# First layer's input projections: queries and keys ahead, then the convolution, then values; heads and latent convolution finished between the blocks

## The reference, cut to what matters

```python
def even_mixer(h_lat, h_ctx, w_in, conv_w, q_g, k_g, rpb, w_out, need_ctx):
    def query_side(p):
        gb, gc, u, q = jnp.split(p, [CONV_CH, 2 * CONV_CH, 3 * CONV_CH], -1)   # 4 x 512
        y_conv = gb * dwconv3(gc * u, conv_w)
        return y_conv, rms_norm(split_heads(q, NA_HEADS), q_g)
    def kv_side(p):
        k, v = jnp.split(p, 2, -1)
        return rms_norm(split_heads(k, NA_HEADS), k_g), split_heads(v, NA_HEADS)
    p_lat = h_lat @ w_in          # 1024 x 3072
    p_ctx = h_ctx @ w_in
    ...
    y_na = merge_heads(neighbourhood_attention(q_lat, k_lat, v_lat, k_ctx, v_ctx, rpb))
    y_na_ctx = merge_heads(dense_attention(q_ctx, k_ctx, v_ctx))
    # both streams: concatenate conv and attention, @ w_out
```

## Time and profile before

| | |
|---|---|
| median of 3 runs | 3195.71 us (3195.0 to 3195.91) |
| the profiled execution | 3196.73 us |
| its span, first to last instruction | 3194.9 us |
| PE / DVE / ACT / POOL busy in it | 88% / 57% / 48% / 5% |
| granted PE clock, mean | 0.93 of 2.4 GHz |
| latent projection, context projection | 57.4 to 150.3 us, 159.8 to 250.3 us |
| first scores of latent attention | 275.70 us |

### The profile page before, as it was taken

One profiled execution on the slowest core, in us unless ns is written; L12 is line 12 of the kernel. 1 busy time (PEld: TensorE's weight loads), 2 busy tenths in 40 slices (PEclk: granted clock), 3 DMA queues, 4 the chain that ended last, 5 costly groups with the idle time before them and its releaser, 6 DMA issues.

```text
span 3194.9 us, 34582 instructions
## 1 busy us (share of the span) xinstructions
PE 2826.9 (88%) x13343; PEld 2335.9 (73%) x13343; DVE 1831.3 (57%) x2220; ACT 1522.7 (48%) x2142; POOL 147.1 (5%) x195
## 2 busy tenths in 40 slices
PE   6897689989975877999999899898689989897798
PEld 5775578878864556888888688677578878787587
DVE  5566556656646444555688755447655555545555
ACT  4553245545534323444677644463444444445344
POOL 1012000000011000000000000000100000100000
PEclk8998889999987786999999999899799999999899
DMA  7662146656662003555799845450045545560354
GB/s 254 230 223 72 53 143 226 211 172 220 214 137 92 1 1 125 178 170 170 238 321 330 292 158 182 135 186 12 7 148 166 193 164 177 182 197 17 99 159 143
DMA packets 266417, 511.15 MB, mean 160 GB/s; under 512 B 9252, under 2 KB 40188, under 8 KB 266267
## 3 DMA queue, kind: packets, MB, share of 16 engines
q1 hardware_dynamic: 262320, 498.11, 46.8%
q0 software_dynamic: 3952, 11.07, 1.7%
HBM read 508.05 MB, written 1.05 MB: 159 GB/s over the span
## 4 chain that ended last, share of the span: by engine, by line
PE 80%; DVE 9%; ACT 5%; DMA 3%; issue 2%; POOL 2%; DVEq 0%; ACTq 0%; POOLq 0%; SPq 0%
PE bank L377 22%; PE bank L378 22%; PE bank L381 21%; PE bank L1061 2%; PE bank L1074 2%; DVE wlo L325 2%; PE bank L2030 2%; ACT whi L321 1%; PE bank L1087 1%; PE bank L746 1%; PE bank L1699 1%; DMA raw<-in_od_w_in 1%; PE bank L465 1%; DMA raw<-in_moe_w 1%; PE bank L1736 1%
## 5 line engine op out<-in xcount | busy, mean ns | idle before, releaser
L325 DVE TENSOR_TENSOR wlo<-raw,whi 128x1024 fp32r<-128x1024 f32 (+1 forms) x1012 | 1196.8, 1199 | 910.6 <-ACT whi L321 906.2
L321 ACT ACTIVATE whi<-raw 128x1024 fp32r<-128x1024 f32 (+1 forms) x1012 | 1037.5, 1039 | 902.4 <-PE bank L381 860.5
L377 PE MATMUL bank<-whi,xhi 128*128 128x512 f32 (+2 forms) x2432 | 935.8, 385 | 36.8 <-DVE wlo L325 17.3
L378 PE MATMUL bank<-wlo,xhi 128*128 128x512 f32 (+2 forms) x2432 | 925.8, 381 | 0.0
L381 PE MATMUL bank<-whi,xlo 128*128 128x512 f32 (+2 forms) x2432 | 924.8, 380 | 0.0
L377 PEld LDWEIGHTS bank<-whi,xhi 128*128 128x128 f32 x2432 | 465.5, 191 | 130.2 <-issue 41.3
L381 PEld LDWEIGHTS bank<-whi,xlo 128*128 128x128 f32 x2432 | 464.5, 191 | 83.0
L378 PEld LDWEIGHTS bank<-wlo,xhi 128*128 128x128 f32 x2432 | 465.8, 192 | 79.8
L377 PE MATMUL bank<-whi,f_hhi 128*128 128x512 f32 x528 | 210.3, 398 | 3.1 <-ACT f_gates L781 3.1
L378 PE MATMUL bank<-wlo,f_hhi 128*128 128x512 f32 x528 | 209.3, 396 | 0.0
L381 PE MATMUL bank<-whi,f_hlo 128*128 128x512 f32 x528 | 209.2, 396 | 0.0
(11 more groups left out here) (449 smaller groups left out, 2692.0 us busy)
## 6 DMA issues: line engine op xcount, KB each, us to landing
raw<-in_ffn_w SPq DMA_DIRECT2D x180, 1024.0 KB, 5.1
raw<-in_moe_w SPq DMA_DIRECT2D x96, 1024.0 KB, 6.0
raw<-in_ada_w SPq DMA_DIRECT2D x48, 1024.0 KB, 5.9
raw<-in_moe_w SPq DMA_DIRECT2D x48, 768.0 KB, 4.6
raw<-in_ev_w_in SPq DMA_DIRECT2D x24, 1024.0 KB, 6.1
raw<-in_ffn_w SPq DMA_DIRECT2D x36, 512.0 KB, 3.6
raw<-in_hyb_w_in SPq DMA_DIRECT2D x18, 1024.0 KB, 5.0
raw<-in_attn_w_qkv SPq DMA_DIRECT2D x18, 1024.0 KB, 5.1
```

The costliest lines, as they stand in the source:

```text
L321: nc.scalar.activation(whole, part, ACT.Copy).then_inc(sem("w_hi"), 1)
L325: nc.vector.tensor_tensor(wlo[s][:, 0:rows, 0:n], part, whole.bitcast(F32), ALU.subtract)\
L377: nc.tensor.matmul(bank[:, 0:n], xk_h, whi[s][:, wk, 0:n], start=first, stop=False)
L378: ins = nc.tensor.matmul(bank[:, 0:n], xk_h, wlo[s][:, wk, 0:n], start=False, stop=last and xl is None)
```

## The change

The order of the six blocks becomes queries, keys, gate, factors, values in both streams, for SP, PE, ACT and DVE alike. The latent heads' squares, sums, roots and gains move from the context projection to the latent one; the context heads' move from behind the projection into it. Their squares go to other buffers (`esq`), and their sums to columns 2 to 65 of `ss`. POOL loads the gains before the context norm. The transposes of latent queries, latent keys, latent products, latent gates, and context keys and queries stand between the blocks of the context projection (`even_ctx_pe`), the copies behind them between ACT's weight halves, the latent conv tiles behind DVE's steps 17 and 18. The context convolution transposes all products before all gates. The number of matmuls, transposes, loads and vector operations is the same.

```diff
+    EV_ORDER = [c * N for c in (3, 4, 0, 1, 2, 5)]
+    SS_E = (2, 34)
+
+    def even_gains_pool(e):
         for i, name in enumerate(("ev_q_g", "ev_k_g")):
             side_load(e, R_E["gqk"][:, i * HD:i * HD + HD], a[name].broadcast_to([P, HD]), "gqk")
         loaded(e, "gqk", 2)
...
+        root_pool(e, "qk_e0", SS_E[0], SS_E[0] + 32, HD, "qk_e:ss0")
...
+    def even_heads_dve(e, st, i):
+
+        if i in (7, 8):
+            even_sums_dve(e, st, i - 7)
+        if i == 11:
+            e.after(f"qk_e{st}:root", "gqk")
+        if 11 <= i < 11 + 2 * NT:
+            t, stage = (i - 11) // 2, (i - 11) % 2
+            (even_root_dve, even_gain_dve)[stage](e, st, t)
+
+    def even_ctx_dve(e, i, outs):
+
+        if i < NT:
+            if i == 0:
+                e.eng.wait_ge(sem("out_done"), outs)
+            gated_dve(e, 0, i)
+        if i == 2:
+            e.put(nc.vector.memset(cT[:, :, 0:1], 0.0))
+            e.link(nc.vector.memset(cT[:, :, TOK + 1:TOK + 2], 0.0), "pads")
+            e.link(nc.vector.memset(qT[HD:P, :, :], 0.0), "even zeros")
+        if i == 5:
+            odd_zeros_dve(e, 0)
+        even_heads_dve(e, 1, i)
+        if i in (17, 18):
+            if i == 17:
+                e.after("convT0")
+            for b in range(2 * (i - 17), 2 * (i - 17) + 2):
+                conv_tile_dve(e, 0, b)
...
+    def even_lat_act(e, i, outs):
+
+        if i in (6, 7):
+            if i == 6:
+                e.eng.wait_ge(sem("out_done"), outs + 3)
+            even_squares_act(e, 0, i - 6)
+
+    def even_ctx_act(e, i, outs):
+
         if i == 4:
...
+            even_q_out(e, 0, T)
+        if i == 6:
+            e.eng.wait_ge(sem("out_done"), outs + 3)
+            e.after("in_e1:x")
+        if i in (6, 7):
+            even_squares_act(e, 1, i - 6)
+        if i == 8:
+            even_k_out(e, 0)
+        if i in (12, 16):
+            (conv_u_act, conv_g_act)[i // 16](e, 0, T)
+        if i == 18:
+            even_k_out(e, 1)
+        if i == 19:
+            even_q_out(e, 1, (G, U, O)[(outs + 10) % 3])
...
+    def even_ctx_pe(e, i):
+
+        rows_ = lambda st: lambda t: p_e[:, st, t, :]
+        if i == 0:
+            e.after("qk_e:0", "late0")
+            e.put(turn_pairs(T, rows_(0), 1536), "qT_ps0")
+        if i == 1:
+            e.after("qT0")
+            e.put(turn_pairs(T, rows_(0), 2048), "kT_ps0")
+        if i == 2:
+            e.after("kT0", "gcu0")
+            e.put(turn_pairs(T, lambda t: tmp[:, t, :], 0), "convU_ps0")
+        if i == 3:
+            e.after("convU0")
+            e.put(turn_pairs(T, rows_(0), 0), "convG_ps0")
+        if i == 4:
+            e.after("convT0", "qk_e:1")
+            e.put(turn_pairs(T, rows_(1), 2048), "kT_ps1")
+            e.eng.wait_ge(sem("out_done"), e.outs.n - 1)
+            e.put(turn_pairs((G, U, O)[(e.outs.n + 1) % 3], rows_(1), 1536), "qT_ps1")
...
+    def conv_pe(e, st):
+
+        e.after(f"gcu{st}")
+        e.put(turn_pairs(psum[4:6], lambda t: tmp[:, t, :], 0), f"convU_ps{st}")
+        e.put(turn_pairs(T, lambda t: p_e[:, st, t, :], 0), f"convG_ps{st}")
...
             e.eng.wait_ge(sem("out_done"), e.outs.n)
-            conv_pe(e, 0)
-            even_qk_pe(e)
...
-                attn_pe(e, ATT0[st], E_ITEMS[st], ready, "qkT1", f"convT{st}", "even zeros", f"odd zeros{st}")
+                attn_pe(e, ATT0[st], E_ITEMS[st], ready, f"qT{st}", "kT0", "kT1", "qT1", f"convT{st}", f"convU{st}",
+                        f"odd zeros{st}")
```

More of the change, by code:

```diff
@@ L614, in after, with blocks, project_load @@
                 self.eng.wait_ge(sem(f"{key}_done"), n)
-    def project_load(ld, w, k, cols_, first=0, extra=None):
-        for i, c0 in enumerate(range(0, cols_, N)):
+    def blocks(cols_, order):
+        return order or range(0, cols_, N)
+    def project_load(ld, w, k, cols_, first=0, extra=None, order=None):
+        for i, c0 in enumerate(blocks(cols_, order)):
             ld.columns(w, k, first + c0, min(N, cols_ - c0))
@@ L623, in project_load, with project_pe @@
                 extra(i)
-    def project_pe(e, s, xs, cols_, tag, extra=None):
-        for c in range(0, cols_, N):
+    def project_pe(e, s, xs, cols_, tag, extra=None, order=None):
+        for i, c in enumerate(blocks(cols_, order)):
             n = min(N, cols_ - c)
@@ L639, in project_pe, with project_act @@
             if extra:
-                extra(c // N)
-    def project_act(e, s, k, cols_, to, extra=None, post=None):
-        for c in range(0, cols_, N):
+                extra(i)
+    def project_act(e, s, k, cols_, to, extra=None, post=None, order=None):
+        for i, c in enumerate(blocks(cols_, order)):
             n = min(N, cols_ - c)
@@ L1246, in even_qk_pe @@
[L1246 to L1271, removed]
@@ new lines, in program, with even_q_out, even_k_out @@
+    halves = lambda ap: ap.rearrange("p (k t) -> p k t", k=2)
+    def even_q_out(e, st, banks):
+        e.after(f"qT_ps{st}", "even zeros")
+        for b in range(2):
+            e.put(nc.scalar.activation(qT[0:HD, 2 * b:2 * b + 2, st * TOK:st * TOK + TOK],
+                                       halves(banks[b][0:HD, :]), ACT.Copy))
+            e.put(nc.scalar.activation(p_e[HD:P, st, b, 1536:2048], banks[b][HD:P, :], ACT.Copy), f"qT{st}")
+    def even_k_out(e, st):
+        e.after(f"kT_ps{st}")
+        for b in range(2):
+            e.put(nc.scalar.activation(kT[:, 2 * b:2 * b + 2, st * TOK:st * TOK + TOK], halves(T[b][:, :]), ACT.Copy),
+                  f"kT{st}")
@@ new lines, in conv_pe, with conv_u_act, conv_g_act @@
+    def conv_pe(e, st):
+        e.after(f"gcu{st}")
+        e.put(turn_pairs(psum[4:6], lambda t: tmp[:, t, :], 0), f"convU_ps{st}")
+        e.put(turn_pairs(T, lambda t: p_e[:, st, t, :], 0), f"convG_ps{st}")
+    def conv_u_act(e, st, banks):
+        e.after(f"convU_ps{st}", "pads")
+        for b in range(2):
+            e.put(nc.scalar.activation(cT[:, 2 * b:2 * b + 2, 1:TOK + 1], halves(banks[b][:, :]), ACT.Copy), f"convU{st}")
+    def conv_g_act(e, st, banks):
+        e.after(f"convG_ps{st}")
+        for b in range(2):
+            e.put(nc.scalar.activation(tmp[:, b, N:2 * N], banks[b][:, :], ACT.Copy), f"convT{st}")
```

141 lines of the change are left out of this document (57 added, 84 removed).

## The result

The changed kernel takes 3174.02 us in the median of 5 runs (3166.65 to 3179.67), and the kernel before, run beside it, 3195.71 (3192.74 to 3199.14, 5 runs). The ratio is 0.9929, with a 95% interval of 0.9914 to 0.9943: 22.7 us less, between 18 and 27. The profiled execution took 3172.25 us (span 3170.3, granted clock 0.93), 24.5 less than the one before.

What follows compares the result with a forecast made beforehand. PE bounds the context projection; behind it, 25.4 us are bound only by operations waiting for each other. -21.4 + 1.25 + 2.4 - 2.3 = -20.0 us gives 3175.7 against the median, forecast as 3176, range 3171 to 3183.

Steps and rivals of the forecast that it cites:

- The gap, -21.4: Between context projection and latent attention: first scores start at 254.34 instead of 275.70, -21.4 us.
- The latent projection, +1.25: Latent projection: the root product of step 13, behind a block's second unit, costs 1.25 us; other moved operations cost nothing.
- The context projection, +2.4: Context projection: transpose groups and DVE operations add 5.65 us, the head work there before saves 3.2, so +2.4.
- The account by DVE's place behind the second unit: Projections: only DVE operations behind a block's second unit cost time; 1.2 + 1.2 + 0.7 make the 3.2 us.
- The context convolution, -2.3: Conv of the context stream: DVE starts 1.1 us earlier and the memset with its wait goes, 1.2; -2.3.
- rival C: Both streams: GpSimd's root holds DVE off for its whole length, +9 us, so 3184.7; chance 0.04.
- B: Within the projections DVE or ACT falls behind, losing 4 to 8 us of the 20: 3180 to 3184; chance 0.13.
- D: Before latent attention the clock survives the shorter idle, saving 2.2 us more: 3173.5; chance 0.07.
- E: Five places where PE waits for ACT's copies or DVE's gains become real waits, each w + 2.2; slower; chance 0.03.
- F: No effect: attention waited for something the chain does not name, only the bias tiles possible; 3195.7; chance 0.03.
- no later stage takes the gain back: Stages after the change: SP's loads wait for free buffers, not for a time, so the -20.0 us stays.

Runs made afterwards that it cites:

- The copies in pairs: Changed kernel with the four query copies grouped (two to qT, then two to e_p) and PE's wait for context queries listed last; one run, 3173.11 us.
- the late copy: Changed kernel with ACT's copies of the latent conv gates at step 17 instead of 16; ratio 0.9929 to the kernel before, 4 runs.

## Why the prediction was right, point by point

**The gap, -21.4.** Right in kind and nearly in size: -20.6. The last copy ends at 254.56 instead of 254.30, since four copies that take turns between `e_qT` and `e_p` follow each other at 0.61, not at the 0.49 taken from copies of 128 partitions; and PE starts 0.42 behind them, not 0.04. The copies in pairs won back a part of both. The clock did not survive the gap: the first scores ran at 0.50, as the sum had it.

**The latent projection, +1.25.** One interval of 17.03, before block 4, the others at 15.75 and 16.38 as before. The stretch grew by only 0.8, because it began nearer to full clock (the first block took 12.8 us instead of 13.3).

**The context projection, +2.4.** Measured +2.3. The intervals are 16.48, 16.92, 16.36, 17.02 and 12.67, where 16.6, 16.7, 16.6, 17.0 and 12.7 were forecast. Eight transposes cost 0.90: the last interval holds two groups and is 1.80 longer than the 10.87 of before. The account by DVE's place behind the second unit was shown by moving it. The projection's end, though, came at 250.21 and not 3.7 later than before: 1.1 less ahead of the latent projection and 2.1 less at the start of the context stream cancel the added work in this pair of executions.

**The context convolution, -2.3.** Measured -2.38, and undone by undoing it.

**The roots (rival C).** Refuted. POOL's two roots and a bias add, from its timeline in the changed kernel:

```profile
99.13 5.47 POOL L690 TENSOR_TENSOR ss<-ss,mhalf 128x32 f32<-128x32 f32 x1
...
202.57 5.46 POOL L690 TENSOR_TENSOR ss<-ss,mhalf 128x32 f32<-128x32 f32 x1
...
213.40 1.28 POOL L1194 TENSOR_TENSOR e_bias<-e_bias,y 128x512 f32<-128x512 f32 x1 [4.45 <-DMA e_bias<-in_k_rpb]
```

DVE's timeline beside the second root and the add:

```profile
202.67 1.24 DVE L325 TENSOR_TENSOR wlo<-raw,whi 128x1024 fp32r<-128x1024 f32 x1 [0.49 <-ACT whi L321]
206.23 5.77 DVE L325 TENSOR_TENSOR wlo<-raw,whi 128x1024 fp32r<-128x1024 f32 x5 [2.32 <-ACT whi L321]
211.91 1.22 DVE L1214 TENSOR_TENSOR e_p<-e_p,ss 128x1024 f32<-128x1024 f32 x1
213.59 2.18 DVE L325 TENSOR_TENSOR wlo<-raw,whi 128x1024 fp32r<-128x1024 f32 x1 [0.46 <-ACT whi L321]
```

The halves at 202.67 and 206.23, inside the root, take their usual 1.2; the one beside the bias add takes 2.18 and ends at 215.77, 1.1 us or nearly a whole operation behind the add's end at 214.68. The root product starts as soon as its step is reached, 3.9 us behind the root (202.57 + 5.46 to 211.91). The rule of the Trainium skill (SBUF — State Buffer, section Who interferes with whom), that such a pair excludes each other for a whole instruction, agrees with the second and not with the first.

**The others.** B did not occur: no group of transposes in the context projection has a wait ahead of it that the profile lists. D did not either: the first scores took 2.05 for two, slow as before; it occurs where the gap is 1.14. E did not, and the late copy shows what it would have cost. F is excluded by the gap itself.

**What the sum lacked.** The table load, -1.3 in this pair and 0.4 to 1.35 by experiment; the context attention, -0.7. With the 0.75 lost in the gap they make the sum -21.3, against 22.7 by the ratio. The prediction looked at the first maximum and stopped there; what follows it had been taken as unchanged. That the 0.75 it had too much in the gap offsets a part of the 2.0 it lacked is chance.

**What is luck in the profiled pair.** It differs by 24.5 us. The start of the context stream gives 2.1 of them, which are not the change's for sure, and 1.1 lie ahead of the latent stream's first matmul: in the thirteen traces it starts between 54.98 and 58.56, in no order by the edits. The lead is 25.2 us at the first feed-forward matmul (437.66 and 412.43) and 24.6 at the end, which looks like the forecast "no later stage takes the gain back" held to 0.6. It does not stay there in between: by the same GpSimd operations in both traces it is 28.0 at 896 us, 21.8 at 1830 and 21.1 at 2574. So stages with the same instructions differ by several us between two executions, and only the medians and the ratio carry the result.

## What to carry to other kernels

A serial stretch between two phases that PE bounds is worth nearly its whole length if its pieces fit into queues that wait anyway. Their price is set by place: a vector operation of 1.2 us was free behind one step and cost its whole length behind another, so look in the timeline for the step at which that engine is the late one. Give each handover the slack of a few us: one copy one step too late lost 3 us of waiting and 3 more of clock.

## What was not expected of the hardware

- The same instructions took 13.36 us in one execution and 11.21 in another, because the granted clock had risen ahead of them or not. In the latent stream, too, the first matmul behind the 32 small ones (L967) takes 0.80 in six of the thirteen traces and 0.50 in seven; in four of the six the small ones are slow too (4.5 to 5.2 us instead of 3.7 to 3.9) and the interval takes 17.9 to 18.0 instead of 16.3 to 16.4. A difference of 2 us between two single profiles, in a stage that holds a change of clock, is no effect of an edit until a second execution shows it.
- With one wait ahead of the first exponential, for the maximum, the activation table load ran ahead of it, in idle time. A second wait there, of ACT for its own last copy, which costs nothing itself, put the 1.28 us of load behind the maximum. Both directions show it; why the load is placed so stays open.
- How long PE stands idle does not settle its clock. An idle time of 1.20 us left it high (the scores behind it took 1.13 for two), and so did one of 1.28; behind one of 1.29 at the same place of another execution, and behind one of 3.09, it was at 0.50.
- ACT's copies of 64 partitions that take turns between `e_qT` (lower 64) and `e_p` (upper 64) start 0.61 us apart; two to one target take 1.06 to 1.08 together, with 0.59 for one. Which of the two turns, the target or the half of the partitions, costs the overlap stays open.
